# One key operand for the recurrence's scores, constants loaded behind the first pieces, and the last rows' output made in two parts of 256 columns

## The reference, cut to what matters

```python
# first block, layer A: x = x + ((u * mixed * silu(z)) @ w_out); u, v, z from rms_norm(x) @ w_in, LN over v
# first block, layer B: 16 heads of banded attention over shared K/V; x = x + (o * silu(z)) @ w_out
# final rms_norm, then the second block:
h = rms_norm_2(x, norm_g);  proj = h @ w_in        # hq, hf, hi, hz, cq, ckv, kr, mz, glog
f = lb + (1 - lb) * sigmoid(hf); q = silu(hq); k = 1 - f; v = hi; log_f = log(f)
b = cumsum(log_f) in chunks of 32;  b_last = b at the chunk's end
q_in, k_in, k_out = q * exp(b), k * exp(-b), k * exp(b_last - b)
scores = tril(q_in @ k_in.T) in each chunk;  o_intra = scores @ v
o_inter = q_in @ state;  state = state * exp(b_last) + k_out.T @ v   # over 16 chunks, 8 heads
y_a = rms_norm_2(o_intra + o_inter, hg_norm_g) * silu(hz)
y_b = causal attention with low-rank q and kv (8 heads, 128 + 64 rotary) * silu(mz)
merged = sigmoid(g0) * (y_a @ w_proj_a) + sigmoid(g1) * (y_b @ w_proj_b)
out = rms_norm_2(x + merged @ w_out, final_norm_g)
```

## Time and profile before

| what | value |
|---|---|
| median of 3 runs | 1306.43 us (1305.44 to 1306.79) |
| the profiled execution | 1304.92 us, of which the span 1303.1 us |
| outside the span in that execution | 1.8 us |
| granted TensorE clock over the span | 0.999 |
| PE busy | 1286.9 us, 99% |
| DVE / ACT / POOL busy | 728.6 / 690.1 / 498.4 us |
| DMA, mean over the span | 102 GB/s |

### The profile page before, as it was taken

How to read it: one execution, slowest core, us unless ns; L and a number is a source line. 1 busy time by engine, 2 the same in 40 slices (tenths; PEclk the granted TensorE clock), 3 DMA queues, 4 the chain that set the end, 5 groups by cost and what they waited for, 6 DMA issues and landing times.

```text
span 1303.1 us, 16288 instructions
## 1 busy us (share of the span) xinstructions
PE 1286.9 (99%) x6349; PEld 1077.0 (83%) x6349; DVE 728.6 (56%) x1286; ACT 690.1 (53%) x1027; POOL 498.4 (38%) x207
## 2 busy tenths in 40 slices
PE   9999999999999999999999999999999999999998
PEld 7888888888887788888877888888878888888886
DVE  5556556561137365565776377777656556642442
ACT  5535544443345567665446577777646555562322
POOL 4453434434444322322445434333333333334530
PEclk9999999999999999999999999999999999999999
DMA  5733322324333232322243322222223222235511
GB/s 183 262 116 97 91 97 84 103 85 161 97 113 96 81 97 64 112 80 64 81 146 118 103 68 65 82 79 68 76 87 99 68 92 73 85 104 195 168 57 64
DMA packets 42588, 132.31 MB, mean 102 GB/s; under 512 B 6992, under 2 KB 9744, under 8 KB 42000
## 3 DMA queue, kind: packets, MB, share of 16 engines
q1 hardware_dynamic: 36416, 115.36, 28.2%
q10 hardware_dynamic: 6096, 15.92, 3.5%
HBM read 124.97 MB, written 10.49 MB: 104 GB/s over the span
## 4 chain that ended last, share of the span: by engine, by line
PE 92%; DVE 5%; ACT 2%; issue 1%; DMA 0%; SPq 0%; DVEq 0%; ACTq 0%
PE banks L505 28%; PE banks L507 28%; PE banks L506 28%; PE banks L686 2%; PE banks L678 1%; PE banks L667 1%; DVE ylo L1702 1%; PE banks L601 1%; PE banks L919 1%; DVE nfull L1698 1%; DVE hlo L1832 0%; DVE nfull L1828 0%; DMA raw<-w 0%; PE banks L951 0%; PE banks L950 0%
## 5 line engine op out<-in xcount | busy, mean ns | idle before, releaser
L495 POOL TENSOR_TENSOR wlo<-raw,whi 128x1024 fp32r<-128x1024 f32 (+2 forms) x198 | 487.3, 2464 | 731.7 <-ACT whi L1070 731.7
L505 PE MATMUL banks<-hhi,whi 128*128 128x512 f32 x752 | 300.3, 399 | 2.5 <-DVE hlo L1832 1.9
L507 PE MATMUL banks<-hlo,whi 128*128 128x512 f32 x752 | 293.5, 390 | 0.0
L506 PE MATMUL banks<-hhi,wlo 128*128 128x512 f32 x752 | 293.4, 390 | 0.0
L1070 ACT ACTIVATE whi<-raw 128x1024 fp32r<-128x1024 f32 (+2 forms) x198 | 205.3, 1038 | 155.7 <-PE banks L507 98.2
L505 PE MATMUL banks<-yhi,whi 128*128 128x512 f32 x448 | 176.5, 394 | 0.2 <-DVE ylo L1702 0.2
L507 PE MATMUL banks<-ylo,whi 128*128 128x512 f32 x448 | 174.7, 390 | 0.0
L506 PE MATMUL banks<-yhi,wlo 128*128 128x512 f32 x448 | 174.4, 389 | 0.0
L505 PEld LDWEIGHTS banks<-hhi,whi 128*128 128x128 f32 x752 | 141.5, 188 | 30.0 <-DVE hlo L1832 3.4
L507 PEld LDWEIGHTS banks<-hlo,whi 128*128 128x128 f32 x752 | 141.2, 188 | 30.3
L506 PEld LDWEIGHTS banks<-hhi,wlo 128*128 128x128 f32 x752 | 141.7, 188 | 25.2
(11 more groups left out here) (382 smaller groups left out, 2160.3 us busy)
## 6 DMA issues: line engine op xcount, KB each, us to landing
raw<-w SPq DMA_DIRECT2D x193, 512.0 KB, 3.5
rel_tab<-relx ACTq DMA_DIRECT2D x1, 4096.0 KB, 21.6
tab<-rel_tab SPq DMA_DIRECT2D x16, 224.0 KB, 3.5
x<-xt ACTq DMA_DIRECT2D x1, 2048.0 KB, 7.8
x_kept<-x ACTq DMA_DIRECT2D x1, 2048.0 KB, 7.4
parts_kept<-mcg SPq DMA_DIRECT2D x8, 256.0 KB, 4.3
mgt<-parts_kept SPq DMA_DIRECT2D x8, 256.0 KB, 3.7
x<-x_kept ACTq DMA_DIRECT2D x1, 2048.0 KB, 7.7
```

Source lines behind the costliest of these rows:

```text
L495: nc.gpsimd.tensor_tensor(lo[:, begin:width], raw[:, n % 2, begin:width], f32(hi[:, begin:width]), ALU.subtract).then_inc(lo_done, 1)
L505: nc.tensor.matmul(dst, a[0], b[0], start=first, stop=False)
L506: nc.tensor.matmul(dst, a[1], b[0], start=False, stop=False)
L507: return nc.tensor.matmul(dst, a[0], b[1], start=False, stop=last)
```

## The change

It has eight parts.

1. **One key operand.** `k_in` and its halves `hks` go. The scores inside a chunk are made with `k_out` (operand `hkos`) and a query operand `qend` = q * exp(b - b_last), which lies behind the crossing queries in `hqxs`. For three of the four blocks of 128 rows both kinds of score are then one `mm3` of 320 columns; the last block keeps 192 and 128 apart, in what two banks have left. The masked copies become eight, three blocks and then the last one, for each kind. exp(-x) now reads `hd` and waits for step `rest`.
2. **Start.** ScalarE makes `yhi` 0 first and then `whi`, `cst` is issued behind them, there are eleven zero products and none behind `first_hi`, and the first round of `v` is ordered by parts: four products high with high, four low with high, four high with low (for later slabs eight of each).
3. **Values.** In the last slab of `av` and `hv` the loop runs over banks outside and k inside (`slab_pairs`), and `at_scores(0)` waits bank by bank.
4. **Last banded head.** ScalarE instead of VectorE makes `hhi` of it.
5. **First recurrence head.** Slabs `hq` 0 and `hf` 0 multiply the tiles before the norm (`y_upper`), and VectorE scales the two banks afterwards by `diag[:, 1, :]`, a copy of the spread 1/rms that ScalarE makes.
6. **Last recurrence head.** VectorE makes `hstlo` before it finishes the head before.
7. **Down projections and second attention.** The row sums go between the k-steps of `g0` 0, VectorE's turn is cut in two around them, ScalarE takes the root before `kp`, and the last head's turning goes behind the first k-step of `g1` 2.
8. **Output.** The last group is two groups of 24 products of 256 columns; the left half's square is summed while the right one is multiplied.

```diff
-            hqxs = [sb(n, [P, TT, HX], F32R, scope) for n in ("hqxhi", "hqxlo")]
+            hqxs = [sb(n, [P, TT, HX + P], F32R, scope) for n in ("hqxhi", "hqxlo")]
-            hks = [sb(n, [P, S], F32R, scope) for n in ("hkhi", "hklo")]
...
-            for n in range(10):
+            for n in range(11):
                 zero_product()
-            pe.wait_ge(first_hi, 1)
-            for n in range(5):
-                zero_product()
+            def first_values(k, a, b):
+                slot, w_cols = k // 2, slice((k % 2) * S, (k % 2 + 1) * S)
+                if (a, b) == (0, 0):
+                    pe.wait_ge(proA.sem, proA.at(f"hi{k}"))
+                    pe.wait_ge(*((first_hi, 1) if k == 0 else (hi_done, slot + 1)))
+                elif a:
+                    pe.wait_ge(proV.sem, proV.at(f"lo{k}"))
+                else:
+                    pe.wait_ge(*((first_lo, 1) if k == 0 else (lo_done, slot + 1)))
...
+            def slab_pairs(j):
+                ks = (2 * j, 2 * j + 1)
+                if j < 3:
+                    return [(k, t) for k in ks for t in range(TT)]
+                return [(k, t) for t in range(TT) for k in ks]
...
                 for t in (1, 2, 0, 3):
+                    if i == 0:
+                        pe.wait_ge(avV.sem, avV.at(f"lo{(2, 1, 2, 3)[t]}", 1))
...
-                    pe.wait_ge(avV.sem, avV.at(f"lo{TT - 1}", 1))
...
-            def hg_diagonal(s, t):
-            def hg_cross(s, t):
+            def hg_block(s, t):
                 if t == 0:
                     pe.wait_ge(hpV.sem, hpV.at("qlo", s))
                     if s >= 1:
-                        pe.wait_ge(htV.sem, htV.at("diag", s - 1))
+                        pe.wait_ge(htV.sem, htV.at("far1", s - 1))
+                keys = [u[:, t * P:(t + 1) * P] for u in hkos]
+                if t < TT - 1:
+                    return mm3(bank[5 + t][:, 0:CROSS + P], keys, [u[:, t, HC:] for u in hqxs], True, True)
+                mm3(bank[5][:, CROSS + P:S], keys, [u[:, t, HC:HX] for u in hqxs], True, True)
+                return mm3(bank[6][:, CROSS + P:CROSS + 2 * P], keys, [u[:, t, HX:] for u in hqxs], True, True)
...
-                slab("hq", r, bank[1], h, between=scores, tiles=n2V if r == 0 else None)
+                slab("hq", r, bank[1], h if r else y_upper, between=scores)
-                slab("hf", r, bank[0], h, between=updates)
+                slab("hf", r, bank[0], h if r else y_upper, between=updates)
...
-            slab("g0", 0, bank[7], h)
+            slab("g0", 0, bank[7], h, between=down_sums)
...
-            ml_turned(MH - 1)
-            slab("g1", 2, bank[3], h)
+            slab("g1", 2, bank[3], h, between=lambda k: ml_turned(MH - 1) if k == 0 else None)
...
-            for at in range(2, KT):
+            for at in range(2, KT - 1):
                 out_group(at)
+            out_group(KT - 1, name="g7left", slabs=slice(0, 2))
+            out_group(KT - 1, name="g7right", slabs=slice(2, TT))
...
-            act.dma_start(cst[:, :], consts).then_inc(ld_cst, 16)
...
+                    if t == 0:
+                        act.wait_ge(ld_first, 16)
+                        nc.scalar.activation(whi[:, 0, 0:S], raw[:, 0, 0:S], ACT.Copy).then_inc(first_hi, 1)
+                        act.dma_start(cst[:, :], consts).then_inc(ld_cst, 16)
...
+                if m == 0:
+                    act.wait_ge(auV.sem, auV.at("y", PAIRS - 1))
+                    nc.scalar.activation(hhi[:, PAIRS - 1, :], ay[:, :], ACT.Copy).then_inc(auH.did("yhi"), 1)
...
-                nc.scalar.activation(hen[:, :], hb[:, :], ACT.Exp, scale=-1.0).then_inc(hpA.did("en"), 1)
                 act.wait_ge(hpV.sem, hpV.at("rest", r))
+                nc.scalar.activation(hen[:, :], hd[:, :], ACT.Exp, scale=-1.0).then_inc(hpA.did("en"), 1)
                 nc.scalar.activation(hd[:, :], hd[:, :], ACT.Exp).then_inc(hpA.did("ed"), 1)
...
+            act.wait_ge(dnV.sem, dnV.at("inv"))
+            nc.scalar.activation(rt3[:, 2, :, :], rt3[:, 1, :, :], ACT.Sqrt).then_inc(dnA.did("root"), 1)
             act.wait_ge(dnV.sem, dnV.at("sum"))
             nc.scalar.activation(mkp[:, 0, :], mt1[:, 0, :], ACT.Copy).then_inc(dnA.did("kp"), 1)
-            act.wait_ge(dnV.sem, dnV.at("inv"))
-            nc.scalar.activation(rt3[:, 2, :, :], rt3[:, 1, :, :], ACT.Sqrt).then_inc(dnA.did("root"), 1)
...
+                if k == 6:
+                    used("hq", 0)
+                    V.tensor_tensor(bank[1], bank[1], diag[:, 1, :], ALU.mult).then_inc(n2V.did("q0"), 1)
+            used("hf", 0)
+            V.tensor_tensor(bank[0], bank[0], diag[:, 1, :], ALU.mult).then_inc(n2V.did("f0"), 1)
...
-                    hg_finish(s - 1)
+                    hg_norm(s - 1)
+                    if s < HH - 1:
+                        hg_finish(s - 1)
                 dve.wait_ge(htA.sem, htA.at("sthi", s))
                 V.tensor_tensor(hsts[1][:, :, :], hst[:, :, :], f32(hsts[0][:, :, :]),
                                 ALU.subtract).then_inc(htV.did("stlo"), 1)
+                if s == HH - 1:
+                    hg_finish(s - 1)
```

330 lines of the change are left out of this document (190 added, 140 removed).

## The result

| | before | after |
|---|---|---|
| median | 1306.61 us (1305.44 to 1308.47, 4 runs) | 1290.49 us (1290.06 to 1291.27, 4 runs) |
| the profiled execution | 1304.92 us, span 1303.1 | 1290.74 us, span 1288.9 |
| granted clock over the span | 0.999 | 0.999 |

The ratio is 0.9876 (95% interval 0.9859 to 0.9893): 1.2% faster, 16.1 us by the medians and 14.2 us by the spans of the two profiles. Of the 3.8 us, 2.1 are terms of the sum (12.1 forecast, 14.2 measured between the profiled executions) and 1.7 come from the step "1.5 for the median": after the change the median is no longer above the profiled execution.

A forecast was written before the change was run, and what follows sets the result against it. The prediction took TensorE's program, busy 99% of the span, as the bound. Its terms summed to 12.1 us off the profiled 1304.92, giving 1292.8, and 1.5 for the median made 1294.3 us; the 8-in-10 range was 1290.5 to 1298.8.

The forecast's parts named there:

- 1.5 for the median: Whole kernel: the median lies 1.5 us above the profiled execution, so 1.5 is added to the forecast of 1292.8.
- the heads' term: Eight recurrence heads: scores with 320-column products gain 4.5 us, less 0.7 for late operands: 3.8, ends 0 and 6.6.
- last banded head: Last head of the banded attention: ScalarE makes the rounding, but GpSimd still holds VectorE's `hlo`; gain 0.3 us.
- first recurrence head: Slabs `hq` 0 and `hf` 0: TensorE no longer waits for the tiles; gain 2.6 us, ends 2.0 and 2.9.
- last recurrence head: Last recurrence head: the whole wait of 1.6 us for `hstlo` goes; gain 1.7 with the restart, ends 1.2 and 1.8.
- down projections: Down projections: the 1.3 us wait goes, but the gate may end last before `pa` 0; 0 taken, ends 1.3 and -0.7.
- rival B: Recurrence heads' scores: a 320-column product costs like one of 384, 0.18 us; 2.2 less gain, 1296.5 us; chance 0.08.
- The start: Kernel start: first real product 1.96 us earlier, about 0.3 lost waiting for the fifth slab; gain 1.7, ends 1.2 and 2.4.
- A: Recurrence heads: ScalarE's delay passes in full and `hqxlo` sets the pace; 1.5 us left instead of 3.8, 1296.6; chance 0.14.
- D: Recurrence heads: VectorE's scan falls behind GpSimd's next `wlo`, about 2.0 us lost a head; slower, 1307.6 us; chance 0.05.
- E: Whole kernel: the change does nothing, TensorE's starts being bound by something all views miss; 1306.4 us; chance 0.01.
- C: Start, gate, heads, last banded head: earlier weights and gate, no stall (0.7 each), 0.5 at the banded head; 1291.7; chance 0.14.

The follow-up runs named there:

- the doubled copies: The changed kernel with the first pair of masked copies made twice in each recurrence head: 1292.79 us, 1.6 above the changed kernel.

## Why the prediction was right and where it was wrong

Two steps carry the 3.8 us by which the forecast missed: the heads' term, 3.8 where 5.8 were measured, and the 1.5 added for the median, where nothing was to be added. The other terms together are right to 0.1 us.

Right: what bounds the kernel, the sign, and that every part but one gains. By terms, forecast to measured: values 1.3 to 1.27, last banded head 0.3 to 0.47, first recurrence head 2.6 to 2.9, last recurrence head 1.7 to 1.76, down projections 0 to -0.13, second attention 0.45 to 0.62, output 0.25 as forecast. The cost of 320 columns, the point of rival B, was right too, and so was the reading that GpSimd holds `hlo`.

Wrong, in the order of size:

- **The heads, 3.8 forecast, 5.8 measured** (undone: 5.8). Two things in the term. It charged a stall of 0.1 a head, 0.7, for late operands; there was none, and the doubled copies show that it begins some 0.4 us later. And it priced the score products alone, 0.56 a head, where a narrow product also slows the wide one behind it: 0.69 against 0.74 us for the next three. The earlier trace rows hold it: from 783.14 to 785.24 are 2.10 us, of which a pair of blocks is 0.62, so six wide products took 1.48, where six at 0.23 are 1.38; I read only the narrow ones. The blocks gained 0.02 to 0.04 a head more than the 0.56, and some 0.02 stand in the six products behind the sums of squares.
- **"1.5 for the median".** I took the distance of one profiled execution to the median as a constant of the measurement and carried it over. It was a property of the kernel before. With its long waits the clock falls in most executions (35 of 43), 1.1 and 1.6 us a time in the profiles, which puts its median 1.3 us above an execution without a dip; the profiled one had happened to keep 1.00, and to lie 0.4 below the median of those. Taking the waits out of the kernel before brought its executions within 0.7 us of each other, and putting them back into the changed one brought the dips back. So a wait of 1.3 us costs its own length, a restart, and now and then as much again, and the change was worth 14.2 us in an execution without dips and 16.1 at the median (15.2 when both ran again).
- **The start, 1.7 forecast, 1.2 measured.** The first product is 2.1 us earlier, about as the step had it (1.96). The fifth slab's `wlo` costs 0.6 with the restart, not 0.3, as ScalarE rounds that slab behind an exponential which waits for VectorE. Another 0.3 went before the row sums, with products that start up to 0.43 us apart, which the step did not have.

The down projections came out at 0 for the reason the step gave, the gate behind `kp` and VectorE's sum. It had not seen that one wait would take the other's place: 1.3 us for the sums became 1.0 for the diagonal, just at the limit that the prediction had set for a new wait. That wait stood behind VectorE's two crossings and the sum, and this could be mended.

None of the rivals A, B, D and E held. C, "more than forecast", had the nearest time, 1291.7, but mostly by luck. Of its reasons the missing stall in the heads held. The last banded head had 0.17 more and not 0.5, the gate did not come earlier, and the first weights' rounding ended 0.35 earlier (6.08 against 6.43) but brought the first product only 0.14 ahead of the forecast. The largest part, the wide products behind narrow ones, C did not have.

## What to carry to other kernels

Price a narrow product with what it does to the next wide one: take the distance from one group's start to the next group's, not the narrow products alone. When the runs of a kernel spread and its profiled execution is at the low end, look at the granted clock of each run, and of the windows behind each long wait, before you carry the difference over to another kernel. A wait that was removed uncovers the next in the same chain; moving what is not needed for it (the crossings, `kp`) out of that chain gave 1.5 us more.

## What the runs showed of the hardware

- TensorE's granted clock fell to 1.2 GHz behind single waits of 1.31 us (with 0.30 right behind it) and 1.59 us, in a program that is busy for 99% of its span: for 3.4 us each time (three profiles), at a cost of 1.1 to 1.6 us. Behind the same wait it fell in one execution and not in another. No dip was seen in a profile behind waits of 1.0 us or less, nor, in five profiles, behind the one of 1.5 us in the banded attention, nor, in four, behind the one of 1.3 in the down projections.
- The distance between products in steady state: 0.11 us at 128 and 192 columns, 0.12 at 256, 0.147 at 320, 0.18 at 384, 0.23 at 512. Three products of 512 columns behind ones of 128 take 0.74 us, behind ones of 320 they take 0.69, as elsewhere.
- A VectorE instruction with two SBUF inputs (`hlo`, 128 x 512) takes 0.69 us alone and 2.04 us beside GpSimd's `wlo`, until 0.55 us behind GpSimd's end.
- Apart from dips, the first 42 us and a slab that lands late near 1200 us, the starts of TensorE's products agree between executions, and between kernels that differ elsewhere, to 0.06 us over hundreds of microseconds. This makes single parts of 0.3 us readable from one profile each, where medians can't tell 0.5.
